# Rebuilding the opening of a two-block transformer kernel: fused norm scale, moved chunk buffers, interleaved token value products and dummy products

## What is computed

```python
sh, sc, gt = _modulation(c, w_mod[i], b_mod[i])
sh_c, sc_c, gt_c = _modulation(c_ctx, w_mod[i], b_mod[i])
h = _rmsnorm(x, pre_g[i]) * (1.0 + sc[:, None, :]) + sh[:, None, :]
hc = _rmsnorm(ctx, pre_g[i]) * (1.0 + sc_c) + sh_c
parts = _split_in(h @ w_in[i])
...
v = _heads(parts[6])
...
kv_c = hc @ w_in[i][:, K_OFF:V_END]
```

## Time and profile before

| | us |
|---|---|
| median of 3 runs | 1702.26 |
| lowest, highest run | 1702.13, 1707.29 |
| span of the profiled execution, first to last instruction | 1703.5 |
| PE busy in it | 1661.9 (98%) |
| first PE instruction | 12.2 after the start |
| last value product on weight job 0 issued | 54.77 |

### The profile page before, as it was taken

How to read it: one execution, slowest core, us unless ns; L and a number is a source line. 1 busy time by engine, 2 the same in 40 slices (tenths; PEclk the granted TensorE clock), 3 DMA queues, 4 the chain that set the end, 5 groups by cost and what they waited for, 6 DMA issues and landing times. The chain is left out here.

```text
span 1703.5 us, 26528 instructions
## 1 busy us (share of the span) xinstructions
PE 1661.9 (98%) x10010; PEld 1408.0 (83%) x10010; DVE 940.9 (55%) x1657; ACT 764.6 (45%) x1326; POOL 631.7 (37%) x439
## 2 busy tenths in 40 slices
PE   6999999999999999999999999999999999999998
PEld 4987777778888889978987788798787788989896
DVE  5326566544445258847546664777545565555552
ACT  5324554532223234566545655444445324535351
POOL 1027767342220086643113332965100227323242
PEclk9999999999999999999999999999999999999998
DMA  7322122133333223345632110224411222222221
GB/s 323 112 88 68 55 74 80 63 129 123 106 116 123 99 83 102 105 179 189 233 119 80 50 50 30 96 100 177 169 50 52 98 99 99 100 99 98 99 100 50
DMA packets 29802, 181.68 MB, mean 107 GB/s; under 512 B 3352, under 2 KB 5784, under 8 KB 10112
## 3 DMA queue, kind: packets, MB, share of 16 engines
q1 hardware_dynamic: 22136, 150.12, 24.5%
q10 hardware_dynamic: 7560, 30.09, 5.1%
HBM read 169.57 MB, written 10.50 MB: 106 GB/s over the span
## 5 line engine op out<-in xcount | busy, mean ns | idle before, releaser
L438 PE MATMUL acc<-rarena,wh 128*128 128x512 f32 (+1 forms) x1720 | 657.7, 382 | 6.9 <-DVE rarena L1792 1.3
L440 PE MATMUL acc<-rarena,wl 128*128 128x512 f32 (+1 forms) x1720 | 642.3, 373 | 0.0
L439 PE MATMUL acc<-rarena,wh 128*128 128x512 f32 (+1 forms) x1720 | 641.9, 373 | 0.0
L438 PEld LDWEIGHTS acc<-rarena,wh 128*128 128x128 f32 x1720 | 323.9, 188 | 87.7 <-issue 23.5
L440 PEld LDWEIGHTS acc<-rarena,wl 128*128 128x128 f32 x1720 | 323.8, 188 | 62.1
L439 PEld LDWEIGHTS acc<-rarena,wh 128*128 128x128 f32 x1720 | 324.2, 188 | 56.4 <-issue 0.5
L320 DVE TENSOR_TENSOR wl<-raw,wh 128x2048 fp32r<-128x2048 f32 x81 | 197.2, 2434 | 239.7 <-ACT wh L314 239.6
L314 ACT ACTIVATE wh<-raw 128x2048 fp32r<-128x2048 f32 x99 | 188.9, 1908 | 76.0 <-PE acc L440 69.4
L2555 POOL TENSOR_TENSOR wl<-raw,wh 128x512 fp32r<-128x512 f32 x78 | 105.0, 1375 | 91.2 <-ACT wh L1330 91.2
L320 POOL TENSOR_TENSOR wl<-raw,wh 128x2048 fp32r<-128x2048 f32 x18 | 82.6, 4591 | 149.4 <-ACT wh L314 149.4
L516 PE MATMUL acc<-wh,rarena 128*128 128x256 f32 x336 | 94.2, 280 | 2.7 <-DVE rarena L1792 2.5
(11 more groups left out here) (346 smaller groups left out, 3083.2 us busy)
## 6 DMA issues: line engine op xcount, KB each, us to landing
raw<-in_w SPq DMA_DIRECT2D x129, 1024.0 KB, 4.8
early<-in_wmod SPq DMA_DIRECT2D x8, 1024.0 KB, 19.8
farena<-in_gate ACTq DMA_DIRECT2D x4, 1024.0 KB, 4.8
mkv_scratch<-rarena ACTq DMA_DIRECT2D x2, 2048.0 KB, 12.0
rarena<-mkv_scratch ACTq DMA_DIRECT2D x1, 4096.0 KB, 15.0
farena<-in_rpb ACTq DMA_DIRECT2D x16, 240.0 KB, 3.8
farena<-in_x_grid SPq DMA_DIRECT2D x2, 1024.0 KB, 6.9
o_scratch<-early ACTq DMA_DIRECT2D x8, 256.0 KB, 2.0
```

The lines of the kernel that those rows point to most:

```text
L438: mm(o, w[0], m[0], start=start, stop=False)
L439: mm(o, w[0], m[1], start=False, stop=False)
L440: return mm(o, w[1], m[0], start=False, stop=stop)
```

## The change

It rebuilds the opening on all five queues.

- DVE: the multiplications of all tiles by the norm (`S[0]`, `S[1]`) are gone. `token_scale` and the new `ctx_scale` do norm and modulation scale in one instruction; the shift moves into `token_hi` (ACT, `Identity` with a bias) and into `token_rows` (DVE, three operands). The tiles are done pair by pair, each pair after its own modulation. The context's fold of squares and its low halves move to POOL.
- Memory: the eight chunk buffers no longer lie on `h`; `mrow` holds 4 rows instead of 8, all rows go through `O[0]`, the columns through `acc[0]` and `acc[1]`. Chunk 7 reuses the buffer of chunk 0, so its load waits until `chunk_rows(0)` has run.
- SP: weight job 0 is loaded before chunk 1, the context after it.
- PE: `keep_warm(n)` makes n dummy products (128 x 128, `ones` by `ones`, never read): 24 at the start, 9 before `chunk_rows(0)`, 17 more up to `chunk_rows(2)`. The token value products are put between the chunks; those of the context come last.

```diff
-        wmod_a = view(early, 0, (8, KT, 256))
-        mrow = view(early, 64, (2 * D,))
+        wmod_a = [view(early, kb, (KT, 256)) for kb in (32, 40, 48, 56, 64)] + \
+            [view(late, 8, (KT, 256)), view(upper, 0, (KT, 256)), view(early, 32, (KT, 256))]
+        mrow = F(25.5, 1024)
...
+            def keep_warm(n):
+                for _ in range(n):
+                    mm(T[1][:, 0:128], ones[:], ones[:], start=True, stop=True)
...
+            pe.wait_ge(s_("consts_ready"), 1)
+            keep_warm(24)
+            pe.wait_ge(s_("consts_ready"), 5)
+            pe.wait_ge(s_("silc_ready"), 4)
+            pe.wait_ge(s_("x_in1"), 16)
+            keep_warm(9)
             chunk_rows(0)
+            keep_warm(6)
             pe.wait_ge(s_("pair_summed"), 1)
             column_sums(S[0], xsq[0][:, 0], 4, True, True).then_inc(s_("acc0_done"), 1)
+            keep_warm(3)
             pe.wait_ge(s_("ncol_ready"), 1)
             spread(S[0], ncol, 4)
             chunk_rows(1)
-            pe.wait_ge(s_("pair_summed"), 2)
-            column_sums(S[1], csq[:, 0], 2, True, True).then_inc(s_("acc0_done"), 1)
+            keep_warm(2)
             chunk_columns(0)
+            keep_warm(6)
             chunk_rows(2)
+            pe.wait_ge(s_("lo_done"), JB["V"] + 1)
+            token_values(0, 2, 3, 4)
+            chunk_rows(3)
+            pe.wait_ge(s_("pair_summed"), 3)
+            column_sums(S[1], csq[:, 0], 2, True, False)
+            chunk_columns(1)
+            column_sums(S[1], csq[:, 1], 2, False, True).then_inc(s_("acc0_done"), 1)
+            chunk_rows(4)
             pe.wait_ge(s_("ncol_ready"), 2)
             spread(S[1], ncol_c, 2)
...
+            token_values(1, 2)
             chunk_rows(5)
-            value_chunk(0)
+            token_values(1, 3)
             chunk_columns(2)
+            token_values(1, 4)
             chunk_rows(6)
+            token_values(2, 2)
             chunk_rows(7)
+            token_values(2, 3)
             chunk_columns(3)
...
+            token_values(2, 4)
...
+            context_values(0)
+            token_values(3, 2, 3, 4)
+            context_values(1)
+            context_values(2)
             pe.wait_ge(s_("seam_ready"), 4)
...
             first_values(5, 0, 4)
+            context_values(3)
...
-                    f(h[0][:, k], x0[:, k], ACT.Copy).then_inc(s_("h_hi"), 1)
+                    act.wait_ge(s_("hf_ready"), SCALED_X[k])
+                    f(h[0][:, k], x0[:, k], ACT.Identity, bias=mods[:, k, 0:1]).then_inc(s_("h_hi"), 1)
...
-                    ts(x0[:, k], x0[:, k], mod_ax[:, k:k + 1], mods[:, k, 0:1], MUL, ADD).then_inc(s_("hf_ready"), 1)
+                    stt(x0[:, k], x0[:, k], mod_ax[:, k:k + 1], S[0][:], MUL, MUL).then_inc(s_("hf_ready"), 1)
...
-                    lo(h[1][:, k], x0[:, k], h[0][:, k]).then_inc(s_("h_ready"), 1)
+                    stt(h[1][:, k], x0[:, k], mods[:, k, 0:1], h[0][:, k].bitcast(f32), ADD, SUB).then_inc(s_("h_ready"), 1)
...
+            gp.wait_ge(s_("sq0_ready"), 3)
+            gt(csq[:, 0:4], csq[:, 0:4], csq[:, 4:8], ADD).then_inc(s_("pair_summed"), 1)
+            gp.wait_ge(s_("pair_summed"), 2)
+            gt(csq[:, 0:2], csq[:, 0:2], csq[:, 2:4], ADD).then_inc(s_("pair_summed"), 1)
...
+                    gt(hc[1][:, k], ctx0[:, k], hc[0][:, k].bitcast(f32), SUB).then_inc(s_("hc_ready"), 1)
```

More of the change, by code:

```diff
@@ L1118, in ctx_hi @@
             def ctx_hi(i):
-                act.wait_ge(s_("mods_ready"), i + 1)
                 for k in (2 * i, 2 * i + 1):
-                    f(ctx0[:, k], ctx0[:, k], ACT.Identity, scale=mod_ac[:, k:k + 1], bias=mods[:, k, 1:2]).then_inc(s_("hcf_ready"), 1)
+                    act.wait_ge(s_("hf_ready"), SCALED_CTX[k])
+                    f(ctx0[:, k], ctx0[:, k], ACT.Identity, bias=mods[:, k, 1:2]).then_inc(s_("hcf_ready"), 1)
                 for k in (2 * i, 2 * i + 1):
@@ L1139, in _ @@
             row_copy(0)
+            split_hi(act, 0, 2, 0)
+            root(0)
+            row_copy(1)
             squares("ctx_in0", csq, ctx0)
[L1141 to L1144 removed]
+            token_hi(0)
             row_copy(2)
             row_copy(3)
+            root(1)
+            row_copy(4)
+            token_hi(1)
+            row_copy(5)
             ctx_hi(0)
[L1148 to L1150 removed]
+            row_copy(6)
+            token_hi(2)
+            row_copy(7)
             ctx_hi(1)
[L1152 to L1157 removed]
+            ctx_hi(2)
+            token_hi(3)
+            ctx_hi(3)
             split_hi(act, 0, 2, JB["V"] + 1)
[L1161 to L1162 removed]
+            for n, gi in enumerate((2, 3, 4, 5, 0, 1)):
+                acc_wait_ready(act, 0, 12, GB["V"] + n)
                 ins = f((Vc[:, gi] if gi < 2 else V[:, gi - 2])[:, 0:JW], V_BANKS[gi][:, 0:JW], ACT.Copy)
@@ L1856, in _ @@
             rms_reciprocal(0)
-            v.wait_ge(s_("sq0_ready"), 3)
-            link(halve(csq, 4))
-            link(halve(csq, 2))
-            halve(csq, 1).then_inc(s_("pair_summed"), 1)
+            modulation(0)
             v.wait_ge(s_("spread_done"), 1)
-            for k in range(KT):
-                if k == 6:
-                    rms_reciprocal(1)
-                last = tt(x0[:, k], x0[:, k], S[0][:], MUL)
-            link(last)
-            v.wait_ge(s_("spread_done"), 2)
-            for k in range(KT):
-                last = tt(ctx0[:, k], ctx0[:, k], S[1][:, 0:CTX], MUL)
-            link(last)
-            modulation(0)
-            modulation(1)
-            token_scale(0)
-            token_scale(1)
-            for i in range(2):
-                ctx_rows(i)
-                token_rows(i)
-            for i in range(2, 4):
-                modulation(i)
-                token_scale(i)
-                ctx_rows(i)
-                token_rows(i)
+            token_scale(0)
+            token_rows(0)
+            rms_reciprocal(1)
+            modulation(1)
+            token_scale(1)
+            token_rows(1)
+            v.wait_ge(s_("spread_done"), 2)
+            ctx_scale(0)
+            ctx_scale(1)
+            modulation(2)
+            token_scale(2)
+            token_rows(2)
+            ctx_scale(2)
+            modulation(3)
+            token_scale(3)
+            token_rows(3)
+            ctx_scale(3)
             v.wait_ge(s_("lo_done"), JB["V"] + 1)
```

88 lines of the change are left out of this document (37 added, 51 removed).

## The result

The changed kernel takes **1713.97 us** (median of 4 runs, 1712.34 to 1715.41) against 1703.85 for the kernel before in the same comparison: a ratio of 1.0056, 95% interval 1.0043 to 1.0070. It is slower, by 10.1 us. The forecast was 1707.2 and its range ended at 1712.0. The profiled execution took 1715.41, the longest of the four, with a span of 1713.7.

The account below looks back on a forecast made before the run. PE was taken as the bound, busy 1661.9 of 1703.5 us. Job 0's last product moves from 54.9 to 59.9, a shift of 4.9 unrounded; added to the median 1702.3 this gives 1707.2, range 1702.5 to 1712.

Parts of the forecast that it names:

- Carry to the end: Behind the opening PE hardly waits, so the shift of weight job 1's start, +4.9, reaches the end whole.
- Start of the chain: Opening up to the first value product: rows at full speed after dummies, first product 8.7 us sooner, at 24.8.
- The part that costs: First pair: DVE's low halves and POOL's fold additions lock shared SBUF ports; second tile starts at 26.5, 1.9 lost.
- the meeting: DVE's first low halves coincide with POOL's additions, each waiting for the other's whole instruction: 1.9 lost.
- the rival without the ports: Ports don't matter here, as POOL's adds come earlier or DVE goes first: +2.6, 1704.9; chance 0.17.
- Rounds A, B, C and tail at full clock: Opening's later pairs, rows to low half, start products at 34.9, 42.8, 50.8; remaining job 0 products end at 59.9.
- blocked `modulation`: In rounds B and C, POOL's context low half blocks modulation's two tiny instructions: 1.1, bounds 0 to 1.2 each.
- The clock: Opening priced with PE at full speed, 2.4 GHz, since PE had kept it across a wait of 1.17.
- The base: Median of the kernel before, 1702.3, to which the shift of 4.9 was added, giving 1707.2.
- clock falls back: Little PE work between 23.3 and 26.5, so half speed until the next round: +4.7, 1711.9; chance 0.13.
- PE never waits once started: From 24.8 PE works through job 0 without waits, ending at 51.0: -3.9, 1698.4, faster than before; chance 0.04.

Follow-up runs that it names:

- experiment 3: Changed kernel with the fold of the context's squares back on DVE instead of POOL, nothing else: 1709.96 us, ratio 1.0036 to the kernel before.
- experiment 1: Changed kernel with 33 more unread dummy products placed in PE's waits, nothing else: 1709.93 us, ratio 1.0035 to the kernel before.
- experiment 12: The kernel before, unchanged, run as the kernel under test against itself: 1703.68 us against 1702.97, ratio 1.0010.
- experiment 6: The kernel before with dummy products alone, at the changed kernel's places and its own order kept: 1707.82 us, ratio 1.0025.
- experiment 2: Changed kernel with only the first two PE waits filled, by nine unread products: 1712.04 us, ratio 1.0054 to the kernel before.
- experiment 4: Changed kernel with both the context's fold back on DVE and the 33 dummy products in PE's waits: 1709.70 us, ratio 1.0034 to the kernel before.
- experiment 11: Changed kernel with fold on DVE, value products between the next pair's rows and columns, and no dummy products: 1710.08 us, ratio 1.0035 to the kernel before.
- experiments 5: Changed kernel without its 50 dummy products, nothing else: 1717.73 us, ratio 1.0077 to the kernel before.

## Why the prediction was wrong

Step by step, as it was put:

- **Carry to the end:** right. Job 1 shifted by 9.7, the span by 10.2.
- **Start of the chain:** right. First product 25.07 for 24.8, rows at full clock from the first chunk. The fused scale took 0.745 a tile (0.74 forecast), the high half with bias 0.716 (0.82, its bounds were 0.62 to 0.82).
- **The part that costs:** right in kind and side, its size too small. Second tile 26.65 for 26.5, but without the meeting it would have been 24.03 (experiment 3), not 24.65: 2.6 for 1.9. The blocked time was met because POOL's additions set it; the open one was 0.6 too late in the sum, mostly where the high halves were priced at 0.87 each and took 0.66 (two in 1.32). Two slips of the sum itself are small: its own terms (25.9 and 0.69) end the second low half at 26.6, not 26.4, and the rival without the ports takes off 2.3 (+2.6 for +4.9) where the wait was worked out as 1.9. The rule of the Trainium skill, "SBUF — State Buffer", section "SBUF: two separate sides", that VectorE and GpSimd hold their shared ports for a whole instruction, fits 4.02 for 1.41, and even 0.80 for 0.23 on 128x2 operands.
- **Rounds A, B, C and tail at full clock:** right. The sum said 34.9, 42.8 and an end at 59.9; experiment 1, with the clock held, gave 34.97, 42.72 and 59.85. Such agreement to 0.1 is partly luck: the blocked `modulation` was put at 1.1 extra in rounds B and C and cost 0.57 and 0.31 (0.31 both times in experiment 1), round C ended at 50.17 for 50.8, and the tail took 9.7 for 9.1, so errors cancelled.
- **The clock: here it failed.** The forecast kept PE at full speed through three rounds whose waits it had itself worked out as about 2 us each, on one row: a wait of 1.17, in a window with 1.92 us of work in 3.00. The changed kernel had 0.64 in 3.1, the clock fell to 0.50 three times, and job 1 started 4.7 us later than with the waits filled (4.0 in the medians). Even the row was one draw: in experiment 12 the kernel before itself loses the clock in a wait of 1.22. The text said that nothing showed a longer wait, and that was a reason for a wide range, not for 0.13. The rival's size, +4.7, was met (4.7), but by another way: it had one fall of one round; the rounds from pair 0 to 1, 1 to 2 and from pair 2 to job 1 were 1.5, 1.6 and 1.5 us longer than in experiment 1. And the second fall stands behind no wait at all, which neither the forecast nor the rival has.
- **Why it got 0.13:** the row on which I doubted the rule of the Trainium skill was the 16 us at half speed with PE mostly busy. That speaks against its second half, the rise after steady work. It says nothing on the first, the fall after an idle stretch (the Trainium skill, "TensorE: Matmul & The Clock Gate", section "HAM oscillation — how this bites in real kernels"), and the falls at 27.1 in the changed kernel and at 23.0 in experiment 6, behind 0.64 us of work in 3.1 and behind a wait of 2.66, agree with that half in kind, though these waits are shorter than the idle stretch that the Trainium skill names there. Those at 34.0 in the changed kernel and at 33.0 in experiment 2, with PE busy before them, do not. Experiment 12 shows that the rise comes at 22.42 in one execution and at 28.8 in another; the single trace could not carry a doubt of either half.
- **The base:** the shift was added to 1702.26, the median of three runs. Those of the kernel before in the four later comparisons, of 15 or 16 runs, are 1702.97 to 1703.68, and it is 1703.85 in this one, of four runs and 1.6 higher. I also took the span, 1703.5, for the time of its execution; in the others the time is 1.7 above the span (1715.41 and 1713.7).

Together, with the clock's part as the traces have it: 4.7 of the clock and 1.6 of the base are 6.3 of the 6.8 us by which the forecast was short; the last 0.5 is within the scatter of a median. The medians divide it otherwise. With the clock held the kernel is 6.7 us above the kernel before (1709.93 and 1703.23), where the traces have 5.0 (59.85 and 54.89), or 5.8 against the 54.04 of experiment 12. So the shift at full clock was right against the one trace that it was worked out from, and 1 to 2 us short against other executions. The rival "clock falls back", on a base of 1703.85, gives 1713.5. "PE never waits once started" was the purpose; it needs products between the rows, and then job 1 starts at 51.79, where that rival had 51.0.

What stays open: why the clock falls after one wait of 1.98 and not after another, why it falls near 33 or 34 us with PE busy (experiment 2), and what puts five of eleven executions of the kernel before near 1707 in one series and one of sixteen in another.

## What to carry to other kernels

When a change moves waits of TensorE from ahead of its work to between its pieces, cost the pieces at half clock too, even where a trace shows full clock across a wait as long, since another trace of the same program may not; and then test it by filling the waits with unread products and nothing else, which separates clock from chain in one run. Fill only real waits: dummies ahead of a product that is ready cost as much as they gave (experiment 4), and dummies behind a wait in which the clock was lost cost more (experiment 6). And count a step that moves from one engine to another with the instructions of both engines that then meet in time.

## What was new about the hardware

- Half clock outlasts the wait in which it starts. In experiment 11 the clock fell in a wait of 2.01 and stayed at 0.50 for 13 us, with PE busy for 11.86 of the 13.40 from 23.8 to 37.2. Without dummies the opening was 3.5 us slower in one order and 6.7 in another (experiments 5 and 11).
- The clock can fall without a wait just before it: in the changed kernel at 34.0, with PE busy 6.84 of the 6.89 us from 27.11 on, and in experiment 2 at 33.0, with 7.72 of 8.00.
- One program's clock differs between executions: full at 22.42 or at 28.8 us, with a fall near 29 or none (experiment 12). A single trace is one draw.
- The blocked instruction need not be large: 128x2 operands waited 0.57 us for POOL's 128x256 ones.
